# The last mixer's channels: convolution projections ahead of the rounds, scores in two PSUM banks, one bank for channels

## What is computed

```python
h = rms_norm_2(x, mix_norm_g)
(u, c_b, c_c, c_x, q, k_c, v_c, k_s, v_s, k_w, v_w, nsa_gates, mix_gates) = split_projection(h @ w_in)
y_ssm  = s5_mixer(u, ...)           # complex linear scan over the tokens, gelu(C x + d u), then a gated product
z      = c_c * c_x                  # short_conv_mixer: product, 3-tap causal convolution per channel,
y_conv = (c_b * conv(z)) @ w_out_c  #   times c_b, product
y_attn = nsa_mixer(q, k_c, ...)     # 8 heads of 64; compressed, selected and windowed attention
gates  = sigmoid(mix_gates)         # 3 x 1024 channels
x = x + (gates[0] * y_ssm + gates[1] * y_conv + gates[2] * y_attn) @ w_out
```

## Time and profile before

| | before |
|---|---|
| median of 3 runs | 1497.79 us |
| the profiled execution | 1497.05 us |
| its span | 1495.2 us |
| TensorE busy, share of the span | 98% |
| VectorE | 77% |
| ScalarE | 52% |
| GpSimd | 10% |
| TensorE in the chain that ended last | 89% |

### The profile page before, as it was taken

One profiled execution on the slowest core, in us unless ns is written; L12 is line 12 of the kernel. 1 busy time (PEld: TensorE's weight loads), 2 busy tenths in 40 slices (PEclk: granted clock), 3 DMA queues, 4 the chain that ended last, 5 costly groups with the idle time before them and its releaser, 6 DMA issues.

```text
span 1495.2 us, 24499 instructions
## 1 busy us (share of the span) xinstructions
PE 1467.2 (98%) x8583; PEld 1274.8 (85%) x8583; DVE 1144.2 (77%) x1833; ACT 770.8 (52%) x1258; POOL 142.5 (10%) x140
## 2 busy tenths in 40 slices
PE   8999999999999999999999999999999999999999
PEld 7888889888888888889878888898877789888887
DVE  5787777877778777787787777778699867567776
ACT  6334376564344543447655443577678655453432
POOL 0000024100000000004120000112323300000000
PEclk9999999999999999999999999999999999999999
DMA  8666555446665666655456665557322256546652
GB/s 315 197 195 196 184 169 169 155 155 197 197 185 193 214 198 196 186 194 171 126 169 200 201 196 184 162 190 232 94 73 84 85 147 189 186 156 194 197 190 82
DMA packets 71361, 261.75 MB, mean 175 GB/s; under 512 B 8048, under 2 KB 8048, under 8 KB 71024
## 3 DMA queue, kind: packets, MB, share of 16 engines
q1 hardware_dynamic: 69984, 253.79, 53.6%
q10 hardware_dynamic: 1296, 6.85, 1.3%
HBM read 259.56 MB, written 1.05 MB: 174 GB/s over the span
## 4 chain that ended last, share of the span: by engine, by line
PE 89%; DVE 5%; ACT 3%; issue 1%; POOL 1%; DMA 0%; ACTq 0%; DVEq 0%
PE work L757 25%; PE work L758 12%; PE acc L472 8%; PE acc L470 8%; PE acc L471 8%; PE work L470 8%; PE work L471 7%; PE work L472 7%; DVE wlo L456 1%; PE work L1482 1%; ACT whi L449 1%; PE acc L1511 1%; PE work L1483 0%; PE acc L1547 0%; DVE frac L1892 0%
## 5 line engine op out<-in xcount | busy, mean ns | idle before, releaser
L456 DVE TENSOR_TENSOR wlo<-raw,whi 128x1024 fp32r<-128x1024 f32 x460 | 549.6, 1221 | 189.6 <-ACT whi L449 188.2
L757 PE MATMUL work<-xboth,whi 128*128 128x512 f32 x1600 | 560.7, 394 | 0.0
L449 ACT ACTIVATE whi<-raw 128x1024 fp32r<-128x1024 f32 x480 | 475.9, 1040 | 53.1 <-PE work L472 35.8
L758 PE MATMUL work<-xboth,wlo 128*128 128x256 f32 x1600 | 444.3, 278 | 0.0
L757 PEld LDWEIGHTS work<-xboth,whi 128*128 128x128 f32 x1600 | 299.8, 187 | 69.2
L758 PEld LDWEIGHTS work<-xboth,wlo 128*128 128x128 f32 x1600 | 300.8, 188 | 4.3
L835 ACT ACTIVATE sg<-sg 128x256 f32<-128x256 f32 x100 | 41.8, 418 | 476.0 <-DVE sg L876 476.0
L472 PE MATMUL acc<-whi,hlo 128*128 128x512 f32 x440 | 173.7, 395 | 0.0
L471 PE MATMUL acc<-wlo,hhi 128*128 128x512 f32 x440 | 173.5, 394 | 0.0
L470 PE MATMUL acc<-whi,hhi 128*128 128x512 f32 x440 | 173.3, 394 | 0.0
L470 PE MATMUL work<-xboth,whi 128*128 128x256 f32 x488 | 142.9, 293 | 0.0
(11 more groups left out here) (437 smaller groups left out, 2095.2 us busy)
## 6 DMA issues: line engine op xcount, KB each, us to landing
raw<-stream SPq DMA_DIRECT2D x480, 512.0 KB, 3.7
par<-pm ACTq DMA_DIRECT2D x2, 1644.5 KB, 7.3
pfa<-pf_a ACTq DMA_DIRECT2D x3, 516.0 KB, 4.6
pfb<-pf_b ACTq DMA_DIRECT2D x2, 516.0 KB, 8.3
x<-x_in SPq DMA_DIRECT2D x2, 512.0 KB, 6.1
out<-x SPq DMA_DIRECT2D x4, 256.0 KB, 2.0
par<-pm ACTq DMA_DIRECT2D x1, 820.0 KB, 4.2
pre<-pf_a ACTq DMA_DIRECT2D x1, 4.0 KB, 4.4
```

The source lines that it names most:

```text
L449: nc.scalar.activation(chunk(whi, place, c)[:, cols], chunk(raw, place, c)[:, cols], ACT.Copy).then_inc(hi_ready, 1)
L456: nc.vector.tensor_tensor(chunk(wlo, place, c)[:, cols], chunk(raw, place, c)[:, cols], chunk(whi, place, c)[:, cols].bitcast(F32), ALU.su ...
L757: nc.tensor.matmul(o[:, :], hi[:, k * P:(k + 1) * P], xboth[:, k, :], start=k == 0, stop=False)
L758: m = nc.tensor.matmul(o[:, 0:S], lo[:, k * P:(k + 1) * P], xhi[:, k, :], start=False, stop=k == KD - 1)
```

## The change

- The eight channels in the setup are now `cv0` to `cv7`, and the rounds have `cv8` to `cv11`, then `e0` to `e11` (`AHEAD = 8`). The work of the convolution on ScalarE and VectorE moves with them.
- The channels of the setup go to the four banks of `acc`; the other steps of the setup rotate through the four W banks alone.
- In the rounds scores take two banks by turns; channels have one.
- ScalarE copies a round's channel right behind the exponentials, ahead of tables and turns.
- `s5_gelu` moves from the end of rounds 4, 8 and 12 to the end of 7, 11 and 15; `s5_low` and the wait of `s5_sum` follow.
- `cv6` stands ahead of `kct`, and `kcn`'s mean ahead of split 35.
- An eighteenth early gate, e17, is projected between the transposes `ot` and the first `lin`; a late gate less.

The core of the diff:

```diff
-EARLY = [(i, b) for i in range(KD) for b in range(3)][:17]
+EARLY = [(i, b) for i in range(KD) for b in range(3)][:18]
+CHANNELS = [f"cv{s}" for s in range(12)] + [f"e{j}" for j in range(len(EARLY))]
+AHEAD = 8
+CHANNEL_CHUNK = [D_MIXED + c for c in (2, 5, 8, 11, 12, 13, 14, 15)] + [D_ROUNDS + c for c in (0, 1, 2, 4, 5, 6, 7, 9, 10, 11, 12, 14, 15, 16, 17, 19)]
+CHANNEL_CHUNK += [D_ROUNDS + c for c in range(20, 26)]
...
+_turns = [name for name in BANKED2 if name not in CHANNELS]
+BANK2 = {name: k % 4 for k, name in enumerate(_turns)}
+BANK2.update((name, 4 + k % 4) for k, name in enumerate(CHANNELS[:AHEAD]))
...
-    BANK2.update(zip(_new + (_cmp[0] + _turn), [SCORES, INPUTS, TURNED]))
-    BANK2.update(zip(_channel + _cmp[1], [SPARE if _r % 2 else CHANNEL, SPARE, TURNED]))
+    BANK2.update(zip(_new + (_cmp[0] + _turn), [SPARE if _r % 2 else SCORES, INPUTS, TURNED]))
+    BANK2.update(zip(_channel + _cmp[1], [CHANNEL, SPARE + 3, SPARE + 2]))
...
+            channel(6)
             begin2(pe, "kct")
             kcn_ready.wait(pe, 1)
             done("kct", nc.tensor.transpose(bank2("kct", slice(0, 16))[0:HD], kcn[0:16, :], ident[0:16, 0:16]))
-            early(6)
             evac2.wait(pe, BY_ACT2.index("kct") + 1)
...
-                if r < 12:
-                    channels(f"cv{r}", D_CONV[r])
-                else:
-                    early(r - 4)
+                channel(AHEAD + r)
...
                 done(f"ot{b}", m)
+            channel(29)
...
+            def conv(i):
+                if i % 3 == 0:
+                    projected(D_CONV[i])
+                    if i:
+                        cz.wait(act, i // 3)
+                    copy(f"cv{i}", cc[:, :], bank2(f"cv{i}", slice(0, S)))
...
                 emptied(f"sc{r}", ins)
-                if 3 <= r <= 12 and r % 3 == 0:
-                    vec2.wait(act, BY_DVE2.index(f"cv{r - 1}") + 1)
-                    cv_hi.inc(nc.scalar.activation(cvhi[:, r // 3 - 1, :], cvt[:, :], ACT.Copy))
...
+                if AHEAD + r < 12:
+                    conv(AHEAD + r)
+                else:
+                    early(AHEAD + r - 12)
                 if t == 0 and h + 1 < 8:
                     tables(h + 1)
...
+                if AHEAD + r in (9, 12):
+                    conv_high((AHEAD + r) // 3 - 1)
                 split_hi(act, place, SPLIT_AFTER[r])
-                if r >= 4 and r % 4 == 0:
+                if r >= 7 and r % 4 == 3:
                     s5_gelu(r // 4 - 1)
...
+            def conv(i):
+                j = i // 3
+                if i % 3 == 1:
+                    dve.wait_ge(consumed, place.count(D_CONV[i]) + RING)
+                    evac2.wait(dve, BY_ACT2.index(f"cv{i - 1}") + 1)
+                    emptied(f"cv{i}", tt(zpad[:, 2:], bank2(f"cv{i}", slice(0, S)), cc[:, :], ALU.mult))
+                    vec2.wait(dve, vec2.k)
+                    cz.inc(ts(cvt[:, :], zpad[:, 0:S], par[:, PN["cw"]][:, 3 * j:3 * j + 1], None, ALU.mult))
+                    cz.wait(dve, j + 1)
+                if i % 3 == 2:
+                    for k in range(1, 3):
+                        step(stt(out=cvt[:, :], in0=zpad[:, k:k + S], scalar=par[:, PN["cw"]][:, 3 * j + k:3 * j + k + 1], in1=cvt[:, :], op0=ALU.mult, op1=ALU.add))
+                    dve.wait_ge(consumed, place.count(D_CONV[i]) + RING)
+                    emptied(f"cv{i}", tt(cvt[:, :], cvt[:, :], bank2(f"cv{i}", slice(0, S)), ALU.mult))
...
-            split_lo(dve, place, range(32, E_CHUNK[4] + 7))
-
+            split_lo(dve, place, range(32, 35))
             evac2.wait(dve, BY_ACT2.index("cmp0") + 1)
...
+            split_lo(dve, place, [35])
+            conv_low(0)
+            conv(4)
+
             nrm.wait(dve, 3)
             job2.wait(dve, JOB2["cmp1"])
...
                 if r + 1 < ROUNDS:
                     front(r + 1)
+                if r % 4 == 0 and r > 4:
+                    s5_low(r // 4 - 2)
                 if r % 4 == 0 and r:
                     s5_sum(r // 4 - 1)
                 if r % 2 == 1 and r < 12:
                     fraction((r + 3) // 2)
-                if r < 12:
...
+                if AHEAD + r < 12:
+                    conv(AHEAD + r)
                 split_lo(dve, place, SPLIT_AFTER[r])
...
+                if AHEAD + r in (9, 12):
+                    conv_low((AHEAD + r) // 3 - 1)
```

More of the change, by code:

```diff
@@ L1406, in mix2_pe, with channel @@
             channels("u3", D_U3)
-            def early(*js):
-                for j in js:
-                    channels(f"e{j}", E_CHUNK[j])
+            def channel(*at):
+                for i in at:
+                    channels(CHANNELS[i], CHANNEL_CHUNK[i])
             def compress(w, half):
@@ L1427, in mix2_pe @@
                     compress(w, half)
-                    early(2 * w + half)
+                    channel(2 * w + half)
             for w in range(2):
@@ L1434, in mix2_pe @@
                 done(f"hidt{w}", m)
-            early(4)
+            channel(4)
             for w in range(2):
@@ L1443, in mix2_pe @@
                 done(f"cmp{w}", m)
-            early(5)
+            channel(5)
             qn_ready.wait(pe, T)
@@ L1471, in mix2_pe @@
                 done(f"cs{t}", m)
-            early(7)
+            channel(7)
             uhl_ready.wait(pe, 4)
@@ L1569, in mix2_pe @@
             turn(15)
-            early(12)
+            channel(24)
             values(15)
-            early(13)
+            channel(25)
             states_out(7)
-            early(14, 15, 16)
+            channel(26, 27, 28)
             combined.wait(pe, 4)
@@ L1715, in early, with ahead, conv_high @@
                     copy(f"e{j}", gates32[j], bank2(f"e{j}", slice(0, S)))
-                    if not 8 <= j < 12:
+                    if j >= 12:
                         split_hi(act, place, [E_CHUNK[j] + 6])
+            def conv(i):
[4 more added lines that the diff above has]
+                    copy(f"cv{i}", cc[:, :], bank2(f"cv{i}", slice(0, S)))
+            def ahead(i):
+                conv(i)
+                split_hi(act, place, [D_CONV[i] + 6])
+            def conv_high(j):
+                vec2.wait(act, BY_DVE2.index(f"cv{3 * j + 2}") + 1)
+                cv_hi.inc(nc.scalar.activation(cvhi[:, j, :], cvt[:, :], ACT.Copy))
             for w in range(2):
                 split_hi(act, place, [c + 6 for c in W1_CHUNK[4 * w:4 * w + 2]])
-                early(2 * w)
+                ahead(2 * w)
                 projected(W1_CHUNK[4 * w + 3])
@@ L1724, in mix2_act @@
                 split_hi(act, place, [c + 6 for c in W1_CHUNK[4 * w + 2:4 * w + 4]])
-                early(2 * w + 1)
+                ahead(2 * w + 1)
             for w in range(2):
@@ L1749, in mix2_act @@
                 cexp.inc(nc.scalar.activation(ce[:, t], ce[:, t], ACT.Exp))
-            early(7)
+            ahead(7)
             def turned_back(p):
@@ L1786, in mix2_act @@
                     turns(h + 2)
-                if r >= 12:
-                    early(r - 4)
-                elif r % 3 == 0:
-                    projected(D_CONV[r])
-                    if r:
-                        cz.wait(act, r // 3)
-                    copy(f"cv{r}", cc[:, :], bank2(f"cv{r}", slice(0, S)))
                 if r == 0:
@@ L1996, in mix2_dve @@
             kcn_ready.inc(stt(out=kcn[0:16, :], in0=kcn[0:16, :], scalar=kc_st[0:16, 1:2], in1=par[0:16, PN["k_g"]][:, 0:HD], op0=ALU.mult, op1=ALU.mult))
-            split_lo(dve, place, range(E_CHUNK[5] + 6, E_CHUNK[6] + 7))
+            split_lo(dve, place, [36])
+            conv(5)
+            split_lo(dve, place, [37])
             for t in range(T):
@@ L2042, in combine @@
                 combined.wait(dve, j + 1)
-            split_lo(dve, place, [E_CHUNK[7] + 6])
+            conv_low(1)
+            split_lo(dve, place, [38])
+            conv(7)
             def front(r):
```

78 lines of the change are left out of this document (36 added, 42 removed).

## The result

| | before | after |
|---|---|---|
| median us (lowest to highest) | 1498.20 (1497.61 to 1499.70), 6 runs | 1505.45 (1503.41 to 1507.99), 6 runs |
| ratio, 95% interval | | 1.0049 (1.0038 to 1.0060) |
| profiled execution, its span | 1497.05, 1495.2 | 1507.99, 1506.0 |

The changed kernel is 7.3 us slower. The forecast was 2.65 us faster and its range ended at 1502: it was wrong in sign and missed its range.

What follows compares the result with a forecast made beforehand. TensorE, busy 1467.2 of 1495.2 us, was taken as the bound, with its waits and lost clock. -0.3 + 9.4 + 4.3 - 12.7 + 1.3 - 4.65 = -2.65 us; 1497.05 - 2.65 + 0.74 gave 1495.1 us, range 1488.5 to 1502.

Steps and rivals of the forecast that it cites:

- Before the rounds: Setup of the second mixer: moved convolution work changes the time by -0.3 us, bounds -5.0 and +2.5.
- I take 0.7 us off the 1.6: Setup: TensorE's 1.6 us wait for `cmp1`'s evacuation shrinks by 0.7 us, earlier work outweighing `cvlo` 0 and conv(4) in front.
- Net -0.3: Setup total: 0.7 us off the `cmp1` wait, +0.4 for `kct`, whose copy no projection hides any more.
- Rounds 1, 3 and 4: Early rounds with one channel bank: TensorE waits for VectorE to empty it, +2.9, +2.0 and +4.5 us, sum +9.4.
- the clock behind them: Early rounds: lowered clock after the three channel-bank waits, 1.7, 0 and 2.6 us, +4.3 in all.
- The order of the fractions in front of conv(11): Round 4: conv(11) stands behind the fractions on VectorE, so the bank empties late: +4.1, +5.0 if slow, 4.5 taken.
- Rounds 5 to 15: Later rounds: 15.6 us of waits and lost clock go, VectorE at 73.3 us then bounds: -12.7, plus 1.3 in round 15.
- The terms named for what VectorE gives back: Last five long-and-short pairs: products of conv(5), (7), (8), (10), (11) and three `cvlo` leave VectorE's 80.2 us, 6.9 us.
- the gain comes from GELU's place: Later rounds: GELU three rounds after `y5t` is summed loses its wait; this, not the scores' bank, brings the gain.
- The second score bank: Later rounds: alone it brings nothing, since transposes behind the scores wait for the same exponentials one step later.
- After the rounds: Between `ot` and `lin0`: gate 17 fills the `olo` wait and the clock stays up, -4.65 us, bounds -2.9 to -4.9.
- The rival on the slower side: Single channel bank in the early rounds costs over 16.4 us, up to 20.1: 1501.5 or 1503.2 us; chance 0.20.

Runs made afterwards that it cites:

- mending the order: Changed kernel, conv(2) moved behind the last S5 coefficient, `cvlo` 0 and conv(4) behind `cmp1`'s evacuation: 1501.86 us; among kernels with GpSimd's root ahead of its products, 1482.64 against 1482.22 unmended.
- second channel bank: Changed kernel with cv9 and cv11 (channels of rounds 1 and 3) projected into another, idle bank; scores keep two banks: 1490.33 us, ratio 0.9958.
- GELU behind `pT`: Kernel before with gate 17 behind `ot` and late GELUs behind the `pT` copies of rounds 7, 11, 15: 1492.14 us; with `cvhi` copies later too, 1489.19.
- `cmp1` first: Changed kernel with setup order mended, another channel bank and GELU after the `pT` copy, plus `cmp1` evacuated ahead of split 35 and the root's wait: 1485.26 us.

## Why the prediction was wrong

*Before the rounds: this is the step that failed.* "I take 0.7 us off the 1.6", "Net -0.3", with +2.5 as the upper bound. It makes 6.0 of the 9.95 us between forecast and result; rounds 5 to 15 make 3.0, the early rounds 0.5. The profiles show +5.7: 2.67 more for `cmp1`'s evacuation, the 0.4 for `kct` that was forecast, and the rest clock (0.75 over the stage instead of 0.84).

Three things were wrong in it. First, the path: the working took the 1.6 for VectorE's own work, but VectorE stood 1.29 us of it for GpSimd's root behind the five products, so that the mean of `kcn` one split earlier could gain nothing. Second, a term that was put at nothing: conv(1) and conv(2) stand ahead of the last S5 coefficient, for which the products wait, and so the root ends 1.7 us later against TensorE's work; moving conv(2) behind it gives most of that back (the first product starts 4.0 us ahead of the first product on `hidT` instead of 2.65). Third, the cost: the instructions moved in front of the evacuation were priced at the length that they have when VectorE works alone. The stretch was named and put only in the bound, for three instructions at the 0.85 of a split; over 1.2, 0.42 and 0.35 us it added 0.6, 0.8 and 1.1 to the split, `cvlo` and `cvt`, and VectorE came 1.4 us after the root. Unstretched they would have ended about a microsecond before the root (an estimate: 2.4 us from 1052.7 on, against 1056.0), and cost nothing. The square, 0.21 us by itself, was stretched in before already, to 1.06; after has 1.30.

Two experiments on this step say that GpSimd's products were the cause, one way or the other: putting them behind the root gave -6.4 with VectorE's order untouched, and with them behind, mending the order gave nothing. How the 6.4 is shared between the stretch and the root's place in GpSimd's queue no run separates; the trace of after gives 1.4 and 1.7 us of waiting. Nor is it shown why the clock behind them is lower: with this setup the same stage took from 23.9 to 26.9 us.

The Trainium skill (SBUF — State Buffer, "Who interferes with whom"), which the prediction cited against this place, was on the right side: the sum by it lay near the upper bound. The trace agrees with it on the evacuation, which has one input in a bank and takes 0.69 us beside a product in after as in before, and on `cvlo` with two in SBUF, 1.26.

*Rounds 1, 3 and 4: right.* Forecast 2.9, 2.0 and 4.5 us, measured 2.73, 1.69 and 3.88; the clock behind them 5.9 instead of 4.3; in all 14.2 for 13.7. The second channel bank shows the cause: the waits and the clock go together. The order of the fractions in front of conv(11) was read rightly.

*Rounds 5 to 15: the mechanism partly right, the size off.* -9.65 for -12.7. No wait for exponentials is left, and `pT` is late in rounds 7, 11 and 15: 1.66, 1.67 and 1.32 us for 1.25, 1.25 and 1.3. The 3 us that are missing are these two sizes (0.8) and the clock behind the first (17.75 is 3.65 over 14.1, of which 1.66 is wait). VectorE, which the sum took for the bound at 73.3 us, was not: it is busy 69.3 of the 76.4 us. (The terms named for what VectorE gives back also add up to 7.1 and not to 6.9.) The reason given, "the gain comes from GELU's place", is false as it stands: alone in the kernel before, that place gave 0.4 us. The change also moved `cvhi` and took work off VectorE; with GELU behind `pT` the place of `cvhi` came out at 3.4. The second score bank was called worth nothing; it came out at 0.7 and 2.5 us, which the intervals do not tell from nothing.

*After the rounds: right in the profile* (-4.4 for -4.65), and 3.1 by the runs.

*The rival on the slower side* had the sign and the wrong place: it wanted the early rounds to cost over 16.4 us, and they cost 14.2. With the setup at its forecast, the change would have been 1.3 us slower (an estimate: 7.3 - 6.0), about the width of the interval.

## What to carry to other kernels

Before a wait is shortened on one engine, read who ended it: here VectorE was itself standing for GpSimd. Before an instruction is moved into a stretch, read which engines are busy there, and price it by its slowest copy beside them; then ask which other engine's work the move shifts against it. When a buffer goes from two to one, list the readers that come late in their engine's queue: each is a wait with a price that the trace of before already gives. A wait that "goes" has to be followed through the queue of the engine that caused it; here the next wait stood one instruction behind.

## What was not expected of the hardware

The same wait does not have the same price in clock. In one profile of the changed kernel the 1.66 us for `pT` in round 7 are followed by a low clock (pair at 0.90, 17.75 us), and the 1.67 in round 11 are not (1.00, 16.35). In one profile an idle gap disappeared and the stage grew no shorter, since the clock was lower later in it (`cmp1` first); whether the one caused the other is not shown, for the clock of this stage differs between profiles of the same code. A microsecond of waiting saved was worth 1.9 us with GpSimd's products behind (6.4 for 3.4), 1.6 with the second channel bank (13.6 for 8.3), and nothing that could be told with `cmp1` first (1.3 us of waiting saved).

A VectorE instruction with its inputs in SBUF, beginning while a GpSimd product of 512 elements per partition ran, was lengthened by up to about the rest of that product, whatever its own size: 16x64 elements took 1.30 us instead of 0.21, and a scaling with one large SBUF input 1.42 instead of 0.35. The other way round GpSimd pays: in after a split begins at 1058.36, a product at 1058.44; the split takes its usual 1.21 us, the product 2.43, where the same product took 1.04 in before.
